# A gated convolution layer on Trainium2: two unused buffers that shift the operands of the wide matmuls to multiples of 512 bytes

## What is computed

```python
def conv_mixer(h, w_in, conv_w, conv_b, ln_g, ln_b, w_out):   # h = rms_norm(x, norm_g)
    z = h @ w_in                                              # 1024 x 3072
    a, b, gate = jnp.split(z, 3, axis=-1)
    u = a * jax.nn.sigmoid(b)
    u = depthwise_causal_conv(u, conv_w, K=31) + conv_b
    uf = layer_norm(u) * ln_g + ln_b                          # over the channels
    u = silu(uf) * silu(gate)
    return u @ w_out                                          # and x is added to it
```

## Time and profile before

| | us |
|---|---|
| median of 3 runs | 363.38 (363.17 to 363.51) |
| the profiled execution, first to last instruction | 361.9 |
| TensorE matmul busy in it | 356.9 (99%) |
| VectorE busy | 319.9 (88%) |
| GpSimd busy | 269.8 (75%) |
| ScalarE busy | 232.4 (64%) |

### The profile page before, as it was taken

The page is one execution under the profiler, slowest core; times in us unless marked ns, Lnnn a source line. Parts: engine busy times, 40 slices in busy tenths (PEclk is TensorE's granted clock), DMA queues, the critical chain, the costliest instruction groups (busy, mean ns, idle before and its releaser), DMA issues.

```text
span 361.9 us, 4758 instructions
## 1 busy us (share of the span) xinstructions
PE 356.9 (99%) x1564; PEld 289.2 (80%) x1564; DVE 319.9 (88%) x514; ACT 232.4 (64%) x334; POOL 269.8 (75%) x194
## 2 busy tenths in 40 slices
PE   7999999999999999999999999999999999999996
PEld 6888888888888888888888888888888888888885
DVE  4779799999999899999999998993798979997952
ACT  5889685558847772998667875975655951452400
POOL 0029999999999997899999999795796532359220
PEclk9999999999999999999999999999999999999999
DMA  7995011201411311406112214235713695066042
GB/s 260 403 400 206 34 60 58 91 28 58 116 60 53 65 60 58 116 2 116 58 60 51 67 58 80 96 58 103 246 59 117 237 404 173 0 203 205 31 169 92
DMA packets 30520, 43.51 MB, mean 120 GB/s; under 512 B 18336, under 2 KB 18848, under 8 KB 30496
## 3 DMA queue, kind: packets, MB, share of 16 engines
q1 hardware_dynamic: 30352, 43.21, 37.7%
q10 hardware_dynamic: 144, 0.00, 0.0%
HBM read 34.82 MB, written 4.19 MB: 108 GB/s over the span
## 4 chain that ended last, share of the span: by engine, by line
PE 97%; DMA 1%; SPq 0%; ACT 0%; DVE 0%; issue 0%
PE mm L632 68%; PE acc L711 12%; PE mm L711 9%; PE mm L649 6%; DMA raw<-w_in 1%; PE acc L702 0%; PE acc L692 0%; PE acc L626 0%; ACT w_hi L786 0%; DVE nat L1273 0%; SPq L494 0%; SPq L520 0%; PE acc L620 0%; PE acc L622 0%
## 5 line engine op out<-in xcount | busy, mean ns | idle before, releaser
L632 PE MATMUL mm<-x_hi,w_hi 128*128 128x512 f32 x352 | 139.3, 396 | 0.0
L632 PE MATMUL mm<-x_hi,w_lo 128*128 128x512 f32 x352 | 139.0, 395 | 0.0
L632 PE MATMUL mm<-x_lo,w_hi 128*128 128x512 f32 x352 | 139.0, 395 | 0.0
L1185 DVE SCALAR_TENSOR_TENSOR acc<-u,chan,acc 128x512 f32<-128x512 f32 x157 | 110.7, 750 | 0.1
L632 PEld LDWEIGHTS mm<-x_hi,w_lo 128*128 128x128 f32 x352 | 66.1, 188 | 16.0
L632 PEld LDWEIGHTS mm<-x_hi,w_hi 128*128 128x128 f32 x352 | 66.1, 188 | 15.8
L632 PEld LDWEIGHTS mm<-x_lo,w_hi 128*128 128x128 f32 x352 | 66.1, 188 | 15.8
L1494 POOL TENSOR_TENSOR pconv<-pconv,prod 128x512 f32<-128x512 f32 x60 | 77.3, 1312 | 1.3 <-ACT prod L868 1.3
L1185 DVE SCALAR_TENSOR_TENSOR acc<-u,w_sum,acc 128x512 f32<-128x512 f32 x90 | 67.5, 750 | 1.3 <-ACT acc L850 1.1
L868 ACT ACTIVATE prod<-u,chan 128x512 f32<-128x512 f32 x69 | 47.7, 714 | 15.6 <-POOL pconv L1494 14.3
L1438 POOL TENSOR_TENSOR w_lo<-raw,w_hi 128x1024 fp32r<-128x1024 f32 (+1 forms) x21 | 49.7, 2365 | 9.3 <-ACT w_hi L817 9.2
(11 more groups left out here) (109 smaller groups left out, 541.2 us busy)
## 6 DMA issues: line engine op xcount, KB each, us to landing
raw<-w_in SPq DMA_DIRECT2D x22, 512.0 KB, 3.3
nat<-x_t SPq DMA_DIRECT2D x16, 256.0 KB, 6.1
sgate<-x SPq DMA_DIRECT2D x8, 512.0 KB, 10.8
raw<-w_out SPq DMA_DIRECT2D x8, 512.0 KB, 3.3
nat<-x SPq DMA_DIRECT2D x8, 512.0 KB, 7.9
y<-nat SPq DMA_DIRECT2D x15, 256.0 KB, 2.1
raw_late<-w_out SPq DMA_DIRECT2D x4, 512.0 KB, 4.1
sig<-w_out SPq DMA_DIRECT2D x4, 512.0 KB, 3.9
```

The lines of the kernel that those rows point to most:

```text
L632: ins = nc.tensor.matmul(bank(("unit", m, h)), w[:, m % 3, k, :], xx[:, k, half(h)], start=(k == 0 and i == 0), stop=(k == KC - 1 and i == 2))
L1185: ins = nc.vector.scalar_tensor_tensor(dst, chain_in(j, chain, k), tap(j, chain, k), chain_bank(j, chain), ALU.mult, ALU.add)
```

## The change

Two buffers of 96 float32 values (384 bytes in each partition) are allocated and never used, one ahead of nat and one ahead of w_hi. Every buffer from nat on moves up by 384 bytes, every one from w_hi on by 768. The instructions, their order and their semaphores are the same.

```diff
+        sb("gap_before_x", [P, 96])
         nat = sb("nat", [P, NT, D])
         x_hi = sb("x_hi", [P, KC, T], F32R)
         x_lo = sb("x_lo", [P, KC, T], F32R)
...
         sig = sb("sig", [P, 2, HALF])
 
 
+        sb("gap_before_w", [P, 96])
         first = ExitStack()
         with first:
             w_hi = sb("w_hi", [P, 3, KC, P], F32R, first)
```

## The result

| | before | after |
|---|---|---|
| median, us | 363.31 (363.17 to 363.51, 4 runs) | 357.50 (356.82 to 358.20, 4 runs) |
| ratio | | 0.9839, 95% interval 0.9826 to 0.9853 |
| profiled execution, span | 361.9 | 356.2 |
| time outside the span | 1.5 (median of the first 3 runs less span) | 1.8 (358.03 less span) |

The change makes the kernel 1.6% faster.

A forecast was written before the change was run, and what follows sets the result against it. TensorE, busy 99%, was taken as the bound: 361.9 us span, +0 for 1478 matmuls, −0.1 for first DMAs, plus 1.5 outside the span, gives 363.3 us; own range 362.7 to 363.7, 8-in-10 range 358.0 to 364.6.

The forecast's parts named there:

- What bounds the kernel: Whole span: TensorE, busy 99%, sets the time through 1478 wide matmuls of 233.3 ns, 20.0 ns of each not columns.
- the first reading under "The wide matmuls": Projection and output product use operands in opposite roles, both at 233.3 ns, so phases 128 or 256 don't matter.
- the term for 1476 matmuls: Change in the wide matmuls' step from the new phases: taken as 0, bounds −4 to +4 ns each.
- The aligned pair: L620 and L622, both operands already on multiples of 512: four steps of 0.92 us, at most 5 ns each.
- The 256 columns: Narrow matmuls at the end, 119.1 ns a step: about 5 ns go with the instruction, about 15 with columns.
- The rival of 512-byte pieces: Wide matmuls: aligned moving slices touch four pieces, not five, saving 4.0 ns each; 358.2 to 360.5 us; chance 0.29.
- The cap on the gain: At the means: TensorE 4.3 us early, VectorE follows by at most 2.3, so this part gives 1.3 to 3.6.
- the case without a wait: If matmuls shorten and TensorE shows no new wait on L692 or the u buffers: time near 357.5 us.
- The other cadence: Wide matmuls all step at 232.4 ns, as in the stretch at 265 us: 1.2 us faster, 362.1; chance 0.04.
- Both streams in one phase (slower): Stationary load and moving stream collide, each wide matmul 237 ns: 5.9 us more, 369.2; chance 0.10, smaller loss 0.04.
- Other engines and DMAs: Shifted operands of other engines cost nothing; first raw DMAs on the chain give −0.1 us, between 0 and −0.2.
- The page's formula: Skill's N/2.4 + 2.5 ns, 215.8 for 512 columns; were misalignment the reason for the excess, 26 us gain, 337 us.

The follow-up runs named there:

- the late spreads alone: The kernel before, without gaps, with only the means and deviations spread later among TensorE's last units: 363.65 us, ratio 1.0009.

## Why the prediction was wrong

- **What bounds the kernel** was right: the gain came through the step of the wide matmuls, and the 20 ns that aren't columns were the place to look. Only the first 0.57 us, by which the first piece of unit 1 was ready earlier, came otherwise; the prediction had 0.1 for it, and the scatter of the starts covers the rest.
- **The step that failed** is the first reading under "The wide matmuls". It saw that the projection (moving 128, stationary 256 past) and the output product (the other way round) step alike, and concluded that the phases don't matter. But exchanging two operands only turns the sign of their difference, and −128 and 128 are the same modulo 256. The comparison was blind to the very quantity that counts. So the term for 1476 matmuls was put at 0 where it measured −6.67 ns each. The walk of the slices by multiples of 512 was rightly read, and for the same reason can't show it: 512 is 0 modulo 256.
- **The aligned pair.** L620 and L622 were the only wide matmuls of the trace with difference 0. I bounded their effect at 5 ns each from four steps that add up to 0.92 us, right behind a stretch of another difference. The steady value is 6.7 ns. Four steps can't show it: in the kernel after, where all differences are 0, the same four take 0.91 us. The hint was on the right side, and I set it at 0 on the strength of the exchange.
- **The 256 columns.** I split the 20 ns into 5 for the instruction and 15 for the columns. After the change the 512-column step has 13.3 ns of surplus and the 256-column ones step by 0.12 us, unchanged or slightly longer than the 119.1 of the earlier trace rows; the last two rows of the kernel after are

```profile
353.04 0.28 PE L713 MATMUL acc<-wb_lo,x_hi 128*128 128x256 f32 x1
353.16 0.28 PE L713 MATMUL acc<-wb_hi,x_lo 128*128 128x256 f32 x1
```

So at a difference of 0 the surplus is 13.3 ns for either width, and the split by columns was wrong. It isn't a fixed cost of the instruction either: at a difference of 64 the narrow ones have 6.8 ns (113.5 above). The rival of 512-byte pieces was fitted to this split; its sign was right, its mechanism wrong (128 past a multiple is as good), and its size, 4.0 ns for 6.67, too small by 40%.
- **The cap on the gain** was right in kind: the wait at the spread of the means is there, where the prediction put it. Its terms were off. TensorE came 7.2 us early, not 4.3, and VectorE followed by 3.6 us (means complete at 253.9 for 257.5), not by 2.3 at most. It didn't have the lower clock behind the wait, 1.7 us in the profiled execution. So 4.9 us came through the wait where the rival had 3.6 at most, 2.5 came behind the means where it had 1.6, and 1.7 went to the clock: 5.7 us for the rival's 5.2, and the time, 357.5, lies 0.7 below the rival's best case. That it equals the 357.5 which the prediction gave for the case without a wait is chance, since the wait is there.
- **The other cadence** isn't tied to the change: the late spreads alone, at a difference of 128, have stretches of the output product at 232.3 ns (48 matmuls in 11.15 us).
- **Both streams in one phase (slower)** had the sign reversed: for 512 columns to coincide is the best case of those tried, and every other one but −64 costs the full 6.7 ns.
- **Other engines and DMAs** were rightly set at nothing: GpSimd's x_lo takes 1,298 ns after for 1,296 in the earlier trace rows, and w_out lands in 3.3, 4.0 and 4.0 us for the 3.3, 4.1 and 3.9 of the earlier trace rows, although by the addresses raw has come onto a multiple of 256 and sig, which the prediction didn't say, has left one.
- **The page's formula.** The formula of the Trainium skill ("TensorE: Matmul & The Clock Gate", section "Back-to-back issue gap") gives 215.8 ns for 512 columns, which the section calls the gap of a single matmul; for a stream of loads and matmuls it has some 131. No run here comes near either: 226.7 is the best of all layouts tried for these 4-byte operands. At the lower clock the section's N/1.2 agrees, 427 ns to 0.43 us measured.

## What to carry to other kernels

Where TensorE streams wide matmuls of 4-byte operands back to back, lay out the stationary and the moving buffers with the same start modulo 256 bytes; of the layouts tried here this was the best for 512 columns, and it is worth 3% of the matmuls' time for a few hundred bytes. With 256 columns another difference was quicker, so measure it for the width in use; other types were not tried. An observation that swaps two things can't tell whether their distance matters: ask of each "it makes no difference" which quantity it holds fixed. When the bounding engine gets faster, move what it waits for along with it; here four changed places in two lists raised the gain from 5.8 to 7.5 us, each against the kernel before on the same chip.

## What was not expected of the hardware

- The distance of two wide matmuls depends on the stationary operand's start minus the moving one's, modulo 256 bytes: 226.7 ns at 0, 228.8 to 228.9 at 192, 233.3 at 32, 64, 128 and 224. Where a difference was tried with several phases (0, 64, 128 and 192), they made no difference.
- With 256 columns the order is another: 113.5 ns at 64, 117.8 at 192 and 224, 118.7 to 119.1 at 128, 119.6 to 120.0 at 0.
- One shifted slice in three lengthens two steps of three, to 232.0 and 234.6 ns, not one.
- With the difference at 0 the surplus of an instruction is the same 13.3 ns for 512 and 256 columns, and at the lower clock the rows show none (0.43 us for 512 columns).
- After a wait of 2.1 to 2.2 us of TensorE the granted clock fell to the lower level in some executions of a kernel and not in others (0.995 in two of four, then in three of four), and it didn't after one of 2.2 and one of 2.7 us in two other kernels.
